# A round's second low-rank product moved up behind its first inverse, its tanh ahead of the group norm's root, and one weighted sum moved back

## The chip, the cores and the metric

The kernel runs on one core of a Trainium2 chip. The time is device microseconds of one execution, and several executions of each kernel are compared by their medians. The engines are TensorE (PE, products), VectorE (DVE), ScalarE (ACT), GpSimd (POOL) and SyncE (SP, which issues transfers). Each works through its own queue in order, and they wait for one another by semaphores.

## The reference

One layer, 512 tokens of 1024 features, 16 heads of 64. Cut to what the change touches:

```python
mod = (silu(c) @ w_ada + b_ada)                       # six vectors of 1024
p = (x * (1 + sc1) + sh1) @ w_in                      # pool, r, k, v, xw, xa, xg, two gates
w = -softplus(-(w0 + tanh(xw) @ w_decay_up)) - 0.5    # low-rank product, decay
a = sigmoid(a0 + xa @ w_aaa_up)                       # low-rank product, a
g = sigmoid(xg) @ w_gate_up
kk = heads(k * k_k); kk = kk / norm(kk)               # root and inverse
k = k * (1 + (a - 1) * k_a)
# per token: S = S*decay + (S @ -kk) (kk*a)^T + v k^T ;  o = S @ r
o = layer_norm(o, gn_g, gn_b, 64e-5)                  # group norm of a head, a root
o = o + sum(r * k * r_k) * v                          # the bonus
y_rwkv = (o * g) @ w_rwkv_up
# then the mix with the pool branch, layer norm, feed-forward (1024 x 4096), layer norm
```

## The kernel before

The heads are worked in four groups of four (QUADS = 4). A group is two halves q = 0 and 1 of 128 features each. The program for the recurrence runs rounds `it` from -1 to 4, each of 27 steps `s`, and each engine has a function `slot(it, s)` that says what it does in that step. The order is written by hand. In a round three groups are under way: `prep` prepares group it + 1 (low-rank products, decay, norms, keys), `work` solves group it in chunks of 64 tokens, and `tail` finishes group it - 1 (group norm, turn, gate). Round -1 only prepares, rounds 1 and 2 do all three, round 3 has no `prep`, round 4 only finishes. Round 0 has no `tail`.

Between these, TensorE runs pieces of the large product with w_in: a piece is 4 multiplies of 128x512 (line 1846), and PER_SLOT says how many pieces follow in each step: 3 in step 8, none in 9, 3 in 10, none in 11, 3 in 12. The weights of that product are split into a high part on ScalarE (line 790) and a low part on GpSimd (line 673); TensorE waits for the low part.

TensorE's results of the recurrence go to three accumulator sets in turn. The list PE_ORDER says in which order, and so which set an item takes (its place in the list modulo 3); an item waits until the one before it in the same set has been taken away.

The names that matter here, in the order of TensorE's steps:

- W0 (step 8), then inv0 (step 8, line 1965), the spread of the inverse norm of half 0, made by VectorE from a root on ScalarE; VectorE uses it in `unit_keys` (line 1313).
- bonus (step 9, line 1983); VectorE takes it at line 1424.
- D (step 10, line 1888).
- lora1 (lines 1947 and 1948), the low-rank products of half 1. ScalarE takes them in `lora_tanh` (lines 852 and 853, into sg and aa_odd), VectorE sums the decays from sg (lines 1294 and 1297).
- K (step 12, line 1900), HD0 and HD1 (step 12, line 1924). VectorE adds one to K, which gives KI (line 1265).
- yT (step 13, line 1900, reads O), the turn of y; ScalarE copies it at line 996.
- norm1 (step 13, line 1955), the root of it on ScalarE (line 860), the inverse on VectorE (lines 1301 and 1304), inv1 on TensorE (step 15, line 1965).

The group norm's root is on ScalarE in step 9 (line 968). Tanh and exponential share one table of functions there, the root is in another, so each change between them has an ACT_TABLE_LOAD.

Beside that, the vectors `mod` of the second half of w_ada are summed on VectorE, eight weighted sums a round (line 1491, the first 1489), in the steps of ADA_USED. Their weights are loaded by ScalarE's queue in the steps of ADA_LOADED (line 909). Odd-numbered tiles share one place and even-numbered ones another, and a load waits until the sum before it in that place is done: the fifth load counted from zero waits for the sum counted three.

The lines that set this:

```python
ADA_LOADED = (1, 5, 7, 9, 12, 12, 14, 15)
ADA_USED = (4, 8, 10, 11, 13, 14, 16, 26)
ADA_COUNT = (1, 2, 1, 3, 2, 4, 3, 5)
```

Of the kernel before, what the change touches and what calls it, by code (L numbers as in the profile page):

```python
# [14 lines left out]
def build(nc, x, c, w_ada, b_ada, w_in, mu_shift, pool_mix, pool_scale, w_pool_up, w0, w_decay_up, a0,  # L15
# [5 lines left out]
    S, D = x.shape[1], x.shape[2]  # L21
# [24 lines left out]
    with ctx:  # L46
# [125 lines left out]
        def flat(t):  # L172
            return t[:, :, :, :].rearrange("p g c t -> p g (c t)")
# [12 lines left out]
        def blocks(t):  # L186
            return Q[:, t * BPT:(t + 1) * BPT, :]

        def flat_blocks(t):
            return blocks(t).rearrange("p b v -> p (b v)")  # L190
# [29 lines left out]
        def over16(m):  # L220
# [2 lines left out]
        QUADS = PAIRS // 2  # L223
        SLOTS = 27
        PE_ORDER = ["TB", "TK", "O", "BR0", "BR1", "lora0", "mod", "AT0", "AT1", "TV", "AD0", "AD1", "A2T", "norm0", "A4", "A4T",
                    "D1", "KR0", "KR1", "A8T", "D2", "W0", "inv0", "bonus", "D", "lora1", "K", "HD0", "HD1", "yT", "norm1", "gate",
                    "inv1", "V1", "K2", "TT", "AP0", "AP1", "MR0", "MR1", "N", "OI", "S1", "S2", "S3", "S4", "S5", "S6"]
        BY_ACT = ["TB", "TK", "LT0", "LT1", "TV", "A2T", "A4T", "D1", "D2", "W0", "D", "K", "HD0", "HD1", "V1", "TT", "AP0", "N", "OI"]
        BY_DVE = ["BR0", "BR1", "AT0", "AT1", "AD0", "AD1", "A2I", "A4", "A4I", "KR0", "KR1", "A8T", "KI", "K2", "AP1", "MR0", "MR1",
# [138 lines left out]
                seen[raw_of[k]] = (k, at + 1)  # L368
        ADA_LOADED = (1, 5, 7, 9, 12, 12, 14, 15)
        ADA_MIDDLE = 4  # L370
        ADA_USED = (4, 8, 10, 11, 13, 14, 16, 26)
        def ada_tile(kt):

            return flat_blocks(c1) if kt in (2, 4, 6) else y[:, KT - 2:KT, :].rearrange("p g t -> p (g t)")
# [391 lines left out]
        def _(act):  # L766
            counts = {}

            def link(ins, name=None):
                key = name or "act_step"  # L770
                counts[key] = counts.get(key, 0) + 1
                ins.then_inc(sem(key), 1)
                act.wait_ge(sem(key), counts[key])
# [137 lines left out]
            def slot(it, s):  # L911
                n = it + 1
                work, prep, tail = 0 <= it < QUADS, n < QUADS, it >= 1
# [55 lines left out]
                if s == 8:  # L969
                    if work:  # L970
                        keep(b6, "D2", it)
                        keep(c6, "W0", it)
                        wait_made(act, "KR1", it)
                    if tail and it < QUADS:
                        act.wait_ge(sem("centred"), it)
                        link(act.activation(flat_blocks(At), flat(O), ACT.Square), "o_squared")
                if s == 10 and prep:
                    squares(it, 1)
                if s == 10 and it == QUADS:
                    act.wait_ge(sem("gate_spread"), 1)  # L980
                    link(act.activation(gate1[:, :], pset[set_of("gate")][:, :, :].rearrange("p g t -> p (g t)"), ACT.Copy, scale=0.5), "gate_row")
                if s == 12:
                    if prep:
                        lora_tanh(it, 1)
                    if work:
                        load_ada(it, ADA_MIDDLE)
                        keep(b1, "K", it)
                        keep_pair(b2, b7, "HD0", it)
                        keep_pair(b2, b7, "HD1", it)
# [790 lines left out]
        def _(pe):  # L1780
# [224 lines left out]
            def slot(it, s):  # L2005
                work, prep, tail = 0 <= it < QUADS, it + 1 < QUADS, it >= 1
# [45 lines left out]
                if s == 8:  # L2052
                    if work:
                        wait_kept(pe, "A4", it)
                        wait_kept(pe, "A4T", it)
                        to_heads("A8T", it, [(b1, b2)])
                        wait_kept(pe, "D1", it)
                        wait_kept(pe, "A4I", it)
                        to_heads("D2", it, [(std(b4), b7)])
                        wait_kept(pe, "KR0", it)  # L2060
                        wait_kept(pe, "KR1", it)
                        wait_kept(pe, "TV", it)
                        to_heads("W0", it, [(c6, c5)])
                    if prep:
                        inverse_norm(it, 0)
                if s == 9 and work:
                    bonus(it)
                if s == 10 and work:
                    wait_kept(pe, "A8T", it)
                    wait_kept(pe, "D2", it)  # L2070
                    to_pairs("D", it, [(std(b5), b6)])
                if s == 11 and prep:
                    lora(it, 1)
                if s == 12 and work:
                    pe.wait_ge(sem("lt_masked"), it + 1)
                    wait_kept(pe, "D", it)
# [278 lines left out]
```

## Time and profile before

| | us |
|---|---|
| median of 3 runs | 1065.74 |
| lowest, highest | 1058.37, 1066.62 |
| profiled execution, its own time | 1067.4 |
| span of the profiled execution | 1065.7 |
| TensorE busy | 976.8 |
| VectorE busy | 677.8 |
| ScalarE busy | 467.0 |
| GpSimd busy | 378.1 |

The rounds lie about so in the span: round -1 from 72 us, 0 from 120, 1 from 212, 2 from 304, 3 from 402, 4 from 497 to 525. Behind them come the gates and up products, the output product and the feed-forward part, which the change does not touch. A number in brackets at the end of a row of a timeline is how long the engine sat idle before it, and who released it.

### The profile page before, as it was taken

Reading aid. Unit: us, or ns where it says so; the run is one execution under the profiler, and the core shown is the slowest. Engines: PE = TensorE matmul, PEld = TensorE weight load, DVE = VectorE, ACT = ScalarE, POOL = GpSimd, SP = SyncE. Lnnn points to the kernel's source line nnn. Section 1 sums busy time; section 2 is a strip of 40 time slices with the busy share of each in tenths; the row PEclk is TensorE's granted clock in tenths of the full one; section 3 lists DMA queues with packets and bytes.
Section 4 is the critical chain, followed back from the end, with each engine's and each line's share of the span. In section 5 each row is a group of like instructions: output and inputs, shape, how many; then the busy total and the mean of one; then the engine's idle time right before and its main releaser. Section 6 shows DMA issues by size and latency. Waiting matters only on the chain.

```text
span 1065.7 us, 27456 instructions
## 1 busy us (share of the span) xinstructions
PE 976.8 (92%) x11539; PEld 811.6 (76%) x11539; DVE 677.8 (64%) x929; ACT 467.0 (44%) x571; POOL 378.1 (35%) x226
## 2 busy tenths in 40 slices
PE   1798898999999899899999999798999999999994
PEld 1676786787768577767688888688898898998983
DVE  5734666658847876683223155467787787787877
ACT  0335354337534632444533243284545445445451
POOL 6332501321231132123544445245153351451532
PEclk9698998999999999999999999988999999999997
DMA  9331323334332333333344337222251432423201
GB/s 365 108 98 45 95 86 89 99 82 117 98 84 85 95 108 82 92 116 81 120 119 108 86 120 231 77 60 79 81 157 36 121 112 65 138 77 85 76 1 79
DMA packets 122919, 108.04 MB, mean 101 GB/s; under 512 B 5395, under 2 KB 104641, under 8 KB 122817
## 3 DMA queue, kind: packets, MB, share of 16 engines
q1 hardware_dynamic: 113009, 83.46, 26.2%
q10 hardware_dynamic: 9808, 23.08, 7.0%
q8 instruction: 81, 1.33, 0.5%
q14 instruction: 21, 0.17, 0.1%
HBM read 100.23 MB, written 2.10 MB: 96 GB/s over the span
## 4 chain that ended last, share of the span: by engine, by line
PE 69%; DVE 17%; ACT 5%; issue 3%; DMA 2%; POOL 2%; SPq 1%; ACTq 0%; DVEq 0%; POOLq 0%
PE bank L1846 12%; PE set L2208 11%; PE bank L2294 7%; PE set L2147 6%; PE bank L2147 5%; PE set L1900 4%; PE set L2294 4%; PE set L2246 3%; PE set L1888 3%; PE set L1912 2%; PE bank L2208 2%; PE bank L1827 2%; DVE a_sum L1516 1%; PE set L1924 1%; DVE w_lo L1557 1%
## 5 line engine op out<-in xcount | busy, mean ns | idle before, releaser
L673 POOL TENSOR_TENSOR w_lo<-w_raw,w_hi 128x1024 fp32r<-128x1024 f32 (+2 forms) x75 | 170.8, 2278 | 393.0 <-ACT w_hi L790 384.6
L790 ACT ACTIVATE w_hi<-w_raw 128x1024 fp32r<-128x1024 f32 (+2 forms) x81 | 81.8, 1010 | 107.3 <-PE set L2147 35.2
L819 ACT ACTIVATE Q<-set 128x1024 f32<-128x1024 f32 x56 | 57.4, 1025 | 138.2 <-PE set L1900 69.3
L1846 PE MATMUL bank<-h_hi,w_hi 128*128 128x512 f32 x256 | 110.3, 431 | 3.4 <-POOL w_lo L673 2.8
L1603 DVE SCALAR_TENSOR_TENSOR res<-set,mod,res 128x256 f32<-128x256 f32 x192 | 92.9, 484 | 26.3 <-PE set L2208 17.5
L2208 PE MATMUL set<-a_hi,w_hi 128*128 128x256 f32 x384 | 109.2, 284 | 0.0
L2208 PE MATMUL set<-a_lo,w_hi 128*128 128x256 f32 x384 | 108.9, 284 | 0.0
L2208 PE MATMUL set<-a_hi,w_lo 128*128 128x256 f32 x384 | 108.9, 283 | 0.0
L1846 PE MATMUL bank<-h_lo,w_hi 128*128 128x512 f32 x256 | 105.1, 411 | 0.0
L1146 ACT ACTIVATE w_hi<-w_raw 128x1024 fp32r<-128x1024 f32 x70 | 74.3, 1062 | 69.8 <-PE set L2208 64.3
L1846 PE MATMUL bank<-h_hi,w_lo 128*128 128x512 f32 x256 | 104.2, 407 | 0.7 <-issue 0.7
L733 POOL TENSOR_TENSOR w_lo<-w_raw,w_hi 128x1024 fp32r<-128x1024 f32 x38 | 91.5, 2408 | 9.8 <-POOL w_lo L733 5.9
L2208 PEld LDWEIGHTS set<-a_hi,w_hi 128*128 128x128 f32 x384 | 74.0, 193 | 0.5
L2208 PEld LDWEIGHTS set<-a_lo,w_hi 128*128 128x128 f32 x384 | 73.9, 193 | 0.3
L2208 PEld LDWEIGHTS set<-a_hi,w_lo 128*128 128x128 f32 x384 | 73.9, 193 | 0.0
L1846 PEld LDWEIGHTS bank<-h_hi,w_hi 128*128 128x128 f32 x256 | 50.1, 196 | 20.4 <-issue 5.9
L740 POOL TENSOR_TENSOR w_raw<-w_raw 128x1024 f32<-128x1024 f32 x8 | 19.4, 2422 | 116.8 <-DVE w_lo L1557 116.8
L1846 PEld LDWEIGHTS bank<-h_hi,w_lo 128*128 128x128 f32 x256 | 49.9, 195 | 11.8 <-issue 0.7
L1846 PEld LDWEIGHTS bank<-h_lo,w_hi 128*128 128x128 f32 x256 | 50.4, 197 | 9.9 <-issue 0.7
L1557 DVE TENSOR_TENSOR w_lo<-w_raw,w_hi 128x1024 fp32r<-128x1024 f32 x38 | 46.6, 1225 | 11.9 <-ACT w_hi L1146 9.2
L2294 PE MATMUL set<-h_hi,w_hi 128*128 128x512 f32 x128 | 49.8, 389 | 0.0
L2294 PE MATMUL set<-h_lo,w_hi 128*128 128x512 f32 x128 | 49.8, 389 | 0.0
(358 smaller groups left out, 2290.3 us busy)
## 6 DMA issues: line engine op xcount, KB each, us to landing
w_raw<-in_w_ff_dram SPq DMA_DIRECT2D x64, 512.0 KB, 4.0
w_raw<-in_w_in_dram SPq DMA_DIRECT2D x46, 512.0 KB, 3.8
y<-in_w_ada_dram ACTq DMA_DIRECT2D x20, 512.0 KB, 3.9
ada<-in_w_ada_dram SPq DMA_DIRECT2D x16, 512.0 KB, 9.9
Q<-in_w_ada_dram ACTq DMA_DIRECT2D x12, 512.0 KB, 4.1
w_raw<-in_w_rwkv_up_dram SPq DMA_DIRECT2D x8, 512.0 KB, 3.7
w_raw<-in_w_out_dram SPq DMA_DIRECT2D x8, 512.0 KB, 4.5
xtok<-in_x_dram SPq DMA_DIRECT2D x4, 512.0 KB, 10.2
```

The lines of the kernel that those rows point to most:

```text
L673: link(pool.tensor_tensor(part_of(k, w_lo), raw_part(k), part_of(k, w_hi).bitcast(F32), ALU.subtract), "lo_ready")
L733: link(pool.tensor_tensor(w_lo[SLOT[m]][:, :, :], raw[:, :, :], w_hi[SLOT[m]][:, :, :].bitcast(F32), ALU.subtract), "lo_ready")
L790: link(act.activation(part_of(k, w_hi), raw_part(k), ACT.Copy), "hi_ready")
L819: link(act.activation(by_half(tile), psum_flat(set_of(name)), ACT.Copy), "act_kept")
L1146: link(act.activation(w_hi[SLOT[m]][:, :, :], raw[:, :, :], ACT.Copy), "hi_ready")
L1557: link(dve.tensor_tensor(w_lo[slot][:, :, :], raw[:, :, :], w_hi[slot][:, :, :].bitcast(F32), ALU.subtract), "lo_by_dve")
L1603: link(dve.scalar_tensor_tensor(out=res[:, f, tokens], in0=product, scalar=mod[:, 40 + f:41 + f], in1=res[:, f, tokens], op0=ALU.mult, op1 ...
L1846: mm = pe.matmul(o, w, hx, start=(m == 0), stop=(m == 3 * KT - 1))
L1900: mm = pe.matmul(ps[N * p:N * p + N, q, c * C:(c + 1) * C], by_pair(left, p, q, c), by_pair(right, p, q, c), start=(m == 0), stop=(m == le ...
L2147: mm = pe.matmul(o, w[slot_of(k)][:, kt, :], hx[:, kt, :], start=(kt == 0 and m == 0), stop=(kt == kts - 1 and m == 2))
L2208: mm = pe.matmul(to, wx[:, i, columns], a[:, form, i, :], start=OPENS[at] and b == 0 and i == 0 and m == 0, stop=i == 1 and m == 2, skip_g ...
L2294: mm = pe.matmul(bank[m][:, :], w[slot][:, kt, :], hx[:, kt, :], start=(kt == 0 and at == 0), stop=(kt == KT - 1 and at == 2))
```

## The change

Three edits, each in the hand-written order.

1. lora1 goes from step 11 to step 8 on TensorE, right behind inv0. With it its place in PE_ORDER changes, so that lora1 takes set 2, bonus set 0 and D set 1 (before: bonus 2, D 0, lora1 1). bonus then waits for W0's copy, D for the use of inv0, K for the tanh pair of lora1, HD0 for the use of bonus, HD1 for D's copy.
2. The tanh pair of lora1 goes from step 12 to the end of step 8 on ScalarE, ahead of the copy and the weight split of step 9, D's copy and the group norm's root.
3. The weighted sum counted three goes from step 11 to step 12 on VectorE, behind KI and the decay sums.

```diff
-                    "D1", "KR0", "KR1", "A8T", "D2", "W0", "inv0", "bonus", "D", "lora1", "K", "HD0", "HD1", "yT", "norm1", "gate",
+                    "D1", "KR0", "KR1", "A8T", "D2", "W0", "inv0", "lora1", "bonus", "D", "K", "HD0", "HD1", "yT", "norm1", "gate",
...
-        ADA_USED = (4, 8, 10, 11, 13, 14, 16, 26)
+        ADA_USED = (4, 8, 10, 12, 13, 14, 16, 26)
...
                     if tail and it < QUADS:
                         act.wait_ge(sem("centred"), it)
                         link(act.activation(flat_blocks(At), flat(O), ACT.Square), "o_squared")
+                    if prep:
+                        lora_tanh(it, 1)
...
                 if s == 12:
-                    if prep:
-                        lora_tanh(it, 1)
                     if work:
...
                     if prep:
                         inverse_norm(it, 0)
+                        lora(it, 1)
...
-                if s == 11 and prep:
-                    lora(it, 1)
```

TensorE in round 0, around the first inverse (L1965), with lora1 (L1947, L1948), K (L1900) and the first HD (L1924); the pieces and the bonus product between are left out:

```order
 L1900 MATMUL set<-Q 64x64 x96
 L1965 MATMUL set<-ident,inverse 64x128 x8
+L1947 MATMUL set<-xwa,lup 128x512
+L1948 MATMUL set<-xwa,lup 128x512
...
-L1947 MATMUL set<-xwa,lup 128x512
-L1948 MATMUL set<-xwa,lup 128x512
 L1900 MATMUL set<-Q 64x64 x32
 L1924 MATMUL set<-Q 64x128 x32
```

lora1 now stands directly behind inv0, and K follows the pieces of step 10 directly.

VectorE in round 0, from the last of the scaled writes (L1340) to the inverse of norm1 (L1301); L1265 is KI, L1491 the weighted sums:

```order
 L1340 TENSOR_TENSOR Q<-t 128x2x256
-L1491 SCALAR_TENSOR_TENSOR y<-y,derived 128x1024
-L1265 TENSOR_TENSOR Q<-set,Q 128x1024
-L1294 TENSOR_SCALAR sg<-sg 128x512
-L1297 SCALAR_TENSOR_TENSOR t<-scanm,sg 128x512
+L1265 TENSOR_TENSOR Q<-set,Q 128x1024
+L1294 TENSOR_SCALAR sg<-sg 128x512
+L1297 SCALAR_TENSOR_TENSOR t<-scanm,sg 128x512
+L1491 SCALAR_TENSOR_TENSOR y<-y,derived 128x1024
 L1491 SCALAR_TENSOR_TENSOR y<-Q,derived,y 128x1024
 L1301 TENSOR_SCALAR norms<-norms 128x8
```

One sum went from ahead of KI to behind the decay sums, and stands next to the sum that follows.

ScalarE in round 1, from the square of the group norm (L976) to the second root (L860); L909 are the loads of weights, L996 the copy of the turn:

```order
 L976 ACTIVATE Q<-O 128x1024
+L852 ACTIVATE sg<-set,derived 128x512
+L853 ACTIVATE aa_odd<-set,derived 128x512
 L796 ACTIVATE G<-bank,derived 128x512
...
-L852 ACT_TABLE_LOAD
-L852 ACTIVATE sg<-set,derived 128x512
-L853 ACTIVATE aa_odd<-set,derived 128x512
...
 L996 ACTIVATE y<-set,params 128x512 x2
-L860 ACT_TABLE_LOAD
 L860 ACTIVATE norms<-set 128x8
```

The tanh pair went ahead of the root of step 9, and two table loads are gone. Round 2 shows the same; in rounds -1 and 0 the pair moves and no load goes.

## Rows read from the trace of the kernel before

**Rows 1.** The page, busy time by engine: us, share of the span, instructions
```profile
PE 976.8 (92%) x11539; PEld 811.6 (76%) x11539; DVE 677.8 (64%) x929; ACT 467.0 (44%) x571; POOL 378.1 (35%) x226
```

**Rows 2.** Waits of TensorE, 72 to 525 us: total us, times, longest us
```profile
PE set L1900 <- DVE Q L1265: 3.9, 3, 2.2
...
PE set L1924 <- ACT aa_odd L853: 2.5, 2, 1.3
```

**Rows 3.** Timeline of TensorE, round 1: start us, us, what, [idle before]
```profile
259.82 0.69 PE L1947 MATMUL set<-xwa,lup 64*128 64x512 f32 x1
...
260.88 1.16 PE L1900 MATMUL set<-Q 64*64 64x64 f32 x64
...
264.18 1.10 PE L1924 MATMUL set<-Q 64*64 64x128 f32 x32 [1.26 <-ACT aa_odd L853]
...
269.10 1.16 PE L1900 MATMUL set<-Q,O 64*64 64x64 f32 x64 [0.82 <-DVE Q L1265]
...
275.29 1.09 PE L1965 MATMUL set<-ident,inverse 128*64 128x128 f32 x16
```

**Rows 4.** Timeline of VectorE, round 1
```profile
255.95 1.22 DVE L1424 TENSOR_TENSOR xvb<-set,xvb 128x1024 f32<-128x1024 f32 x1 [1.69 <-PE set L1983]
...
266.40 1.28 DVE L1491 SCALAR_TENSOR_TENSOR y<-y,derived 128x1024 f32<-128x1024 f32 x1
267.72 1.22 DVE L1265 TENSOR_TENSOR Q<-set,Q 128x1024 f32<-128x1024 f32 x1
...
270.70 1.28 DVE L1491 SCALAR_TENSOR_TENSOR y<-Q,derived,y 128x1024 f32<-128x1024 f32 x1
```

**Rows 5.** Timeline of ScalarE, round 1
```profile
261.43 1.28 ACT L852 ACT_TABLE_LOAD   x1
262.72 0.69 ACT L852 ACTIVATE sg<-set,derived 128x512 f32<-128x512 f32 x1
...
267.83 0.34 ACTq L909 DMA_DIRECT2D y<-in_w_ada_dram  x1
270.32 1.59 ACT L996 ACTIVATE y<-set,params 128x512 f32<-128x512 f32 x2 [2.51 <-PE set L1900]
```

**Rows 6.** Timeline of three engines, round 0, from the bonus product on
```profile
169.07 1.23 DVE L1424 TENSOR_TENSOR xvb<-set,xvb 128x1024 f32<-128x1024 f32 x1 [4.98 <-PE set L1983]
...
179.14 0.34 ACTq L909 DMA_DIRECT2D y<-in_w_ada_dram  x1
...
179.56 1.28 ACT L860 ACT_TABLE_LOAD   x1 [0.45 <-ACT Q L825]
...
180.82 1.28 DVE L1491 SCALAR_TENSOR_TENSOR y<-Q,derived,y 128x1024 f32<-128x1024 f32 x1
...
182.60 1.09 PE L1965 MATMUL set<-ident,inverse 128*64 128x128 f32 x16 [1.96 <-DVE inverse L1304]
...
184.40 1.30 DVE L1491 SCALAR_TENSOR_TENSOR y<-y,derived 128x1024 f32<-128x1024 f32 x1 [1.86 <-DMA y<-in_w_ada_dram]
```

**Rows 7.** Timeline of TensorE, round -1, and one operation of GpSimd in it
```profile
88.53 0.79 PE L1846 MATMUL bank<-h_hi,w_hi 128*128 128x512 f32 x1 [1.99 <-POOL w_lo L673]
...
92.02 0.39 PE L1846 MATMUL bank<-h_hi,w_lo 128*128 128x512 f32 x1
...
95.78 0.69 PE L1947 MATMUL set<-xwa,lup 64*128 64x512 f32 x1
...
90.55 2.67 POOL L673 TENSOR_TENSOR w_lo<-w_raw,w_hi 128x1024 fp32r<-128x1024 f32 x1 [2.07 <-ACT w_hi L790]
```

**Rows 8.** Timelines of VectorE and TensorE, round 3, before the turn
```profile
454.59 1.28 DVE L1491 SCALAR_TENSOR_TENSOR G<-y,derived,G 128x1024 f32<-128x1024 f32 x1
...
458.40 1.36 PE L1900 MATMUL set<-Q,O 64*64 64x64 f32 x64 [2.23 <-DVE Q L1265]
```

**Rows 9.** Stretches: us, busy us (instructions) of each engine, TensorE's granted clock, DMA share, GB/s
```profile
88.50:90.00 1.50, 1.47 (x4) 1.18 (x5) 1.23 (x3) 1.44 (x3) 0.00 (x0) 0.50 0.15 32
...
458.40:459.50 1.10, 1.10 (x61) 1.00 (x64) 1.03 (x3) 0.00 (x0) 0.00 (x0) 1.00 0.77 242
```

## The prediction

> **What bounds the kernel now.** I read the share of busy time first, then the waits of TensorE over the stretch with the rounds, then the timelines of single rounds. The span is TensorE's: it is busy 92% of it [rows 1]. What the change can win is therefore idle time of TensorE in the rounds -1 to 4, between 72 and 525 us, and two lines of its waits there bear on the moved code [rows 2]: 3.9 us for VectorE's Q, and 2.5 us for the tanh in aa_odd, the wait that the moved product is about. The timelines decide whether it goes or only turns into another.
>
> Round 1 shows how these waits hang together (round 2 repeats it within 0.1 us). TensorE idles 1.26 us before the second half of HD, and 0.82 us before the turn of y [rows 3]. The first idle waits for aa_odd, which ScalarE makes late because it has just taken a root and must load a table first [rows 5]. The second waits for KI on VectorE, the operation at 267.72 [rows 4]. VectorE itself started that run of work at 255.95, after waiting 1.69 us for the bonus product of TensorE, and works from there almost without a gap to the end of KI [rows 4]. So between the bonus product and the turn, VectorE is what TensorE ends up waiting for, and VectorE's run starts with the bonus product.
>
> **The change, part by part.** The second low-rank product takes 1.06 us of TensorE (259.82 to the next product at 260.88) [rows 3]. It isn't removed: it moves ahead of twelve weight multiplies and the bonus product. So the bonus product comes 1.06 us later, and VectorE's run with it. The weighted sum that moves behind KI takes 1.32 us with its gap (266.40 to 267.72) [rows 4], and leaves the run ahead of KI by as much.
>
> *Rounds 1 and 2.* KI moves 1.06 us later and 1.32 us earlier: 0.26 us earlier. TensorE arrives at the turn 1.26 us sooner, since the tanh is now long done, and waits there 0.82 + 1.26 - 0.26 = 1.82 us in one piece. The gain is 0.26 us in each round, not 2. The two tables that go in each of these rounds (the one before the tanh is at 261.43 [rows 5]) are ScalarE's time, and ScalarE has a new wait in their place. Its fifth transfer of weights, issued at 267.83 [rows 5], overwrites the tile that the moved sum reads. It now stands until that sum is done, which is when the next sum can begin: 270.70 before [rows 4], and 1.06 later by the bonus product, 271.76. Behind it in ScalarE's queue are the turn's copy (270.32) and the second root. The copy starts at 272.1, 1.8 us later; the table load of 1.28 us behind it is gone; so the root is 0.5 us later. Between the turn's start at 269.10 and the second inverse product at 275.29 TensorE has its own products without a gap [rows 3], of which the inverse needs the first two only; a root 0.5 us later is covered by them. Two rounds: -0.5 us.
>
> *Round 0.* Here there is no group norm, so no table is saved. VectorE waited 4.98 us for the bonus product, started at 169.07 and was held by nothing until its sum at 180.82 was done, at 182.10; TensorE idled 1.96 us for the inverse that followed, and began the second inverse product at 182.60, 0.5 us behind VectorE's sum [rows 6]. With the bonus product 1.06 us later the sum starts at 181.88, the moved one having just ended. Only then may ScalarE issue the fifth transfer, before at 179.14; behind it stands the table load for the root, before at 179.56. Transfer, load and root take 0.34 + 1.28 + 0.2, to 183.7 [rows 6], and 0.5 us later, at 184.2, TensorE resumes: +1.6. The same transfer was used 5.26 us after its issue (179.14 to 184.40); now it lands at 187.1, and VectorE loses 2.7 us there. Bounds: +1.06 (only the bonus product counts) and +2.7 (the late transfer counts whole). TensorE is itself 1.6 later and has weight multiplies behind the inverse product, so I take +1.6, the sum of the rows in between.
>
> *Round -1.* After the first inverse product TensorE idles 1.99 us for a low half on GpSimd (88.53) [rows 7]. The moved product fits into it: -1.06. Some 0.95 us of idle are left, no more than the 0.82 and 1.26 us that changed no clock in round 1. Before, the clock fell: the granted clock is 0.50 behind 88.5 us, 1.2 of 2.4 GHz [rows 9]. Eight multiplies from 88.53 to 92.02 took 3.49 us, the sixteen from there to 95.78 took 0.235 each, so the low clock cost 3.49 - 1.88 = 1.6 us [rows 7]. Against that, the tanh pair (0.69 us each [rows 5]) now stands ahead of the high half from which the next low half is made; that one began at 90.55, took 2.67 us [rows 7], and now ends at 94.6, where TensorE would want it at 88.53 + 24 x 0.235 = 94.2. Sum: -1.06 - 1.6 + 0.4 = -2.2 us. If the clock falls all the same it is -1.06, and with no clash at the low half -2.7. I take -2.2, since the idle that stays is nearest to those that cost nothing.
>
> *Round 3.* No product is moved (no round follows that needs it). Only the sum of 454.59 goes behind KI. TensorE idled 2.23 us before the turn, for KI [rows 8]; what was last there comes 1.28 us sooner, so -1.3 us. Bounds: -1.3, and 0 should another wait stand right behind it. I take -1.3, as the 2.23 us are longer than what leaves.
>
> The accumulator sets that change hands have no price of their own: the bonus product now waits for W0 to be copied, D for the first inverse to be used, K for the tanh pair. Between W0 and the bonus product stand two small products and twelve multiplies, some 5 us by the steps above; the other two are older still. Gone, that cover would cost at most what one such wait did, 1.26 us a round. On SyncE's queue the reload of the low-rank weights waits for the moved product, which now comes sooner.
>
> Sum: -2.2 + 1.6 - 0.5 - 1.3 = -2.4 us. Against the profiled execution's own 1067.4 that is 1065.0. That execution lies 1.7 us above the median of the runs, 1065.74; for the median it gives **1063.3 us**. What a measurement can tell from no change is about 1%, 1055.1 to 1076.4.
>
> **Rivals.** *The single idle drops the clock (slower).* In rounds 1 and 2 two idles of 1.26 and 0.82 us become one of 1.8 us before the turn. Behind 1.99 us in round -1 the clock went to 0.50 and cost 1.6 us [rows 7, 9]. Twice that is +3.2, which gives 1066.5, and 1067.6 where round -1 keeps its low clock too. It decides where the multiplies behind the turn run at 1.2 GHz. Against it: in round 3, before the same turn, 2.23 us of idle left the clock at 1.00 [rows 8, 9]. The Trainium skill (TensorE: Matmul & The Clock Gate, What's actually happening) has the clock follow how busy the engine was of late, not one wait alone; that 1.99 us fell and 2.23 us did not agrees. Chance 0.2.
>
> *VectorE has slack.* If its run could start without the bonus product, rounds 1 and 2 would win all their idle, 2 x 2.08 us, and round 0 would lose nothing: -2.2 - 4.2 - 1.3 = -7.7, 1058.0. VectorE's waits of 1.69 and 4.98 us for exactly that product speak against it [rows 4, 6]. Chance 0.1.
>
> *The tables count.* Four loads go. If ScalarE set the pace there, each would return 1.28 us: -5.1, 1060.6. Against it: TensorE's waits for aa_odd are 2.5 us in all [rows 2], and what the tables give is taken by the wait for the reload. Chance 0.05. The Trainium skill (ScalarE: Activation LUTs, What ACT_TABLE_LOAD costs) puts a switch at 2.66 us, its drain counted; by that this rival would give 1055.1. In this trace the tanh starts 1.29 us after its load does [rows 5], and shows no drain.
>
> *Nothing to be seen.* The order is as the change says, but stalls that come and go (the runs lie between 1058.37 and 1066.62) cover it: 1065.7. Chance 0.1. The forecast has the remaining 0.55.
>
> **The numbers.** The cases lie between 1058.0 and 1067.6; with the spread of the runs at the upper end I take 1057.5 to 1068.0 for 8 in 10. Faster by over 1% needs -10.7 us, which VectorE's slack reaches only with a lucky median: 0.05. Slower by over 1% needs +10.7 us, more than the clock falling in every round: 0.03. Within 1%: 0.92.
>
> **What would show it.** Right: in rounds 1 and 2 no idle before HD and one of about 1.8 us before the turn, released by VectorE; ScalarE's copy of the turn directly behind the fifth transfer; in round 0 about 3.5 us of idle before the second inverse product instead of 1.96; in round 3 0.9 us before the turn instead of 2.23; round -1 at full clock behind 88.5 us. Wrong: if the idle before the turn vanishes, VectorE was not what binds; if round 0's second inverse product is not later, ScalarE's wait for the reload costs nothing; if the clock is at 0.5 behind the turn in rounds 1 and 2, the first rival holds.

## The result and the profile after

| | before | after |
|---|---|---|
| median of 20 executions each, us | 1065.29 (1057.74 to 1072.29) | 1073.86 (1066.27 to 1080.13) |
| ratio, with its 95% interval | 1 | 1.0081 (1.006 to 1.0102) |
| profiled execution and its span, us | 1067.4, 1065.7 | 1072.69, 1071.0 |
| mean granted clock of TensorE, profiled execution | 0.964 | 0.962 |
| the same, mean over executions | 0.972 (94, run beside the experiments) | 0.963 (20) |

The change makes the kernel 0.8% slower, by 8.6 us of median. That is less than the 1% that I had set as the bound of no change, but it is outside my range of 1057.5 to 1068.0, and on the wrong side: I had forecast 2.4 us less. (The comparison leaves out executions that lie far above the fastest of their kernel, three of the eleven in e4 below.) The profiled execution of before has a lower clock than its executions mostly have, and the two profiles differ by 5.3 us only.

The page of the kernel after looks like that of before [rows 1]: the same instructions in TensorE, four fewer in ScalarE (the tables), and hardly more busy time.

```profile
PE 979.6 (91%) x11539; PEld 811.0 (76%) x11539; DVE 678.5 (63%) x929; ACT 462.2 (43%) x567; POOL 383.0 (36%) x226
```

The wait of TensorE for KI over the rounds, 72 to 535 us (total us, times, longest), answers to [rows 2]:

```profile
PE set L1900 <- DVE Q L1265: 5.0, 3, 2.1
```

The wait for the tanh is gone, as intended; that for VectorE's KI has grown from 3.9 to 5.0 us and sits in the turn of y. The rounds 1 and 2 on TensorE (start us, us, what, [idle before]) answer to [rows 3]:

```profile
266.67 1.16 PE L1900 MATMUL set<-Q,O 64*64 64x64 f32 x64 [2.05 <-DVE Q L1265]
...
273.89 2.19 PE L1888 MATMUL set<-Q 64*64 64x64 f32 x128
...
364.99 1.96 PE L1900 MATMUL set<-Q,O 64*64 64x64 f32 x64 [2.06 <-DVE Q L1265]
...
378.50 3.69 PE L1888 MATMUL set<-Q 64*64 64x64 f32 x128
382.12 0.50 PE L1846 MATMUL bank<-h_hi,w_hi 128*128 128x512 f32 x1
```

These are the rows to look at. Both rounds have the same idle in the same place, 2.05 and 2.06 us. In round 1 the turn and what follows it take about what they took before: 7.22 us from the turn to the next group of 64x64 products, as before, and 2.19 us for that group (2.09 before). In round 2 every duration in that stretch is nearly twice as long: 13.51 us to the group, and 3.69 us for it. The stretches show why (us, busy us and instructions of PE, PEld, DVE, ACT and POOL, granted clock, DMA share, GB/s):

```profile
268.00:272.00 4.00, 4.00 (x15) 1.73 (x15) 2.88 (x4) 1.86 (x4) 0.00 (x0) 1.00 0.32 91
...
364.99:382.12 17.13, 17.13 (x224) 10.55 (x224) 8.96 (x10) 6.46 (x10) 2.75 (x1) 0.50 0.36 102
...
382.00:384.00 2.00, 2.00 (x16) 1.58 (x10) 1.64 (x2) 0.69 (x1) 0.00 (x0) 0.96 0.71 172
```

The granted clock is 0.50 (1.2 of 2.4 GHz) from the turn at 364.99 to the first weight multiply at 382.12: 17.13 us. I call such a change from 1.00 to 0.50 a fall of the clock. TensorE is busy all that time: the same products take 9.34 us in round 1, from the turn at 266.67 to the weight multiply at 276.01. The next two views show the rest of round 1 on VectorE and on ScalarE (its queue's own rows are ACTq), which answer to [rows 4, 5]:

```profile
254.85 1.22 DVE L1424 TENSOR_TENSOR xvb<-set,xvb 128x1024 f32<-128x1024 f32 x1 [2.78 <-PE set L1983]
...
265.30 1.22 DVE L1265 TENSOR_TENSOR Q<-set,Q 128x1024 f32<-128x1024 f32 x1
```

```profile
269.65 0.34 ACTq L909 DMA_DIRECT2D y<-in_w_ada_dram  x1
270.04 1.59 ACT L996 ACTIVATE y<-set,params 128x512 f32<-128x512 f32 x2 [3.34 <-DVE y L1491]
271.66 0.18 ACT L860 ACTIVATE norms<-set 128x8 f32<-128x8 f32 x1
```

VectorE waits 2.78 us for the bonus product instead of 1.69, that is 1.09 longer (forecast 1.06), and KI starts 10.45 us behind the start of its run instead of 11.77. ScalarE's copy of the turn comes directly behind the fifth transfer, 3.37 us behind the turn's start instead of 1.22, and the root follows without a table. In round 0 the same transfer holds the root, its table load included (ScalarE, TensorE and VectorE, to [rows 6]):

```profile
176.14 0.33 ACTq L909 DMA_DIRECT2D y<-in_w_ada_dram  x1
...
176.56 1.28 ACT L860 ACT_TABLE_LOAD   x1 [3.37 <-DVE y L1491]
...
178.59 1.98 PE L1965 MATMUL set<-ident,inverse 128*64 128x128 f32 x16 [3.71 <-DVE inverse L1304]
...
179.84 2.86 DVE L1491 SCALAR_TENSOR_TENSOR y<-y,derived 128x1024 f32<-128x1024 f32 x1 [1.30 <-DMA y<-in_w_ada_dram]
```

TensorE's idle there is 3.71 us instead of 1.96, and it too goes with a low clock (the second inverse product takes 1.98 us instead of 1.09; the clock is at 0.50 from 177.2 to 184.2, where the kernel before had it low only behind that place, for about half as long). Round -1 went as forecast: the low half is waited for 0.94 us instead of 1.99, and the clock stays (to [rows 7, 9]).

```profile
87.89 0.50 PE L1846 MATMUL bank<-h_hi,w_hi 128*128 128x512 f32 x1 [0.94 <-POOL w_lo L673]
...
100.14 1.09 PE L1965 MATMUL set<-ident,inverse 128*64 128x128 f32 x16 [2.11 <-DVE inverse L1304]
```

```profile
88.00:90.00 2.00, 2.00 (x9) 1.66 (x10) 1.85 (x4) 1.94 (x3) 0.00 (x0) 1.00 0.40 99
...
178.60:182.00 3.40, 3.40 (x72) 3.07 (x76) 2.16 (x1) 3.06 (x4) 2.36 (x1) 0.50 0.11 46
```

In round 3 the idle before the turn is what I said (to [rows 8]):

```profile
463.59 1.25 PE L1900 MATMUL set<-Q,O 64*64 64x64 f32 x64 [0.91 <-DVE Q L1265]
```

Where the time went in the profiled execution is read off the bonus product, which starts once a round. Before it stood at 167.07, 253.96, 351.06 and 444.41; now:

```profile
162.34 1.88 PE L1983 MATMUL set<-G,ones_head 128*128 128x512 f32 x4
...
252.86 1.88 PE L1983 MATMUL set<-G,ones_head 128*128 128x512 f32 x4
...
351.17 1.88 PE L1983 MATMUL set<-G,ones_head 128*128 128x512 f32 x4
...
450.94 1.88 PE L1983 MATMUL set<-G,ones_head 128*128 128x512 f32 x4
```

The kernel after is 4.7 us ahead in round 0, 1.1 ahead in round 1, 0.1 behind in round 2 and 6.5 behind in round 3. Of the 4.7 us, 2.0 are the first idle of round -1, which the forecast has, and 0.6 were there ahead of it. The other 2.1 come behind it and are luck of these two executions for the most part: the idle before the second inverse product of round -1 is 2.11 us in both, but only before did the clock fall there (1.98 us for the product, and 0.50 behind it; after, 1.09 us at 100.14). Before:

```profile
102.76 1.98 PE L1965 MATMUL set<-ident,inverse 128*64 128x128 f32 x16 [2.11 <-DVE inverse L1304]
```

The 3.6 us lost from round 0 to round 1 hold the longer wait for the root and the clock behind it. The 6.4 us lost from round 2 to round 3 hold the clock's fall in round 2.

### The profile page after: what moved, and what is told of

Same layout as the page of the kernel before. It is cut to its first block, busy times and chain, and to the rows that moved or that the text cites. A ratio compares the mean times of both kernels' runs of the same rounds, so it can differ in the third digit from the quotient of the medians.

```text
span 1071.0 us, 27451 instructions
## 1 busy us (share of the span) xinstructions
PE 979.6 (91%) x11539; PEld 811.0 (76%) x11539; DVE 678.5 (63%) x929; ACT 462.2 (43%) x567; POOL 383.0 (36%) x226
## 4 chain that ended last, share of the span: by engine, by line
PE 66%; DVE 19%; ACT 6%; issue 4%; POOL 2%; DMA 2%; SPq 1%; ACTq 0%; DVEq 0%; POOLq 0%
PE bank L1846 11%; PE set L2207 11%; PE bank L2293 7%; PE set L2146 6%; PE bank L2146 5%; PE set L2293 4%; PE set L1900 3%; PE set L2245 3%; PE set L1888 2%; PE bank L2207 2%; PE set L1912 2%; PE bank L1827 2%; DVE a_sum L1516 1%; DVE Q L1265 1%; PE set L1924 1%
## 5 line engine op out<-in xcount | busy, mean ns | idle before, releaser
L1846 PE MATMUL bank<-h_hi,w_hi 128*128 128x512 f32 x256 | 108.1, 422 | 5.3 <-POOL w_lo L673 2.8
L2207 PE MATMUL set<-a_lo,w_hi 128*128 128x256 f32 x384 | 108.6, 283 | 0.0
L2207 PE MATMUL set<-a_hi,w_lo 128*128 128x256 f32 x384 | 108.6, 283 | 0.0
```

Source lines behind the costliest of these rows:

```text
L1846: mm = pe.matmul(o, w, hx, start=(m == 0), stop=(m == 3 * KT - 1))
L2207: mm = pe.matmul(to, wx[:, i, columns], a[:, form, i, :], start=OPENS[at] and b == 0 and i == 0 and m == 0, stop=i == 1 and m == 2, skip_g ...
```

## The experiments

Two theories stood against each other, with two rivals. **The clock:** two short idles that were harmless became one of 2 us, and behind it TensorE falls to half its clock for the whole stretch of products up to the next weight multiplies. **The reload:** ScalarE, held by the fifth transfer, delays the root and the copies behind it. **The tables** and **VectorE's slack** are the rivals of the prediction. A ratio is against the kernel before on the same chip; its median there was 1067.2 for e1 to e4, 1064.85 for e5 to e8, and 1064.98 for e9 to e12. Line numbers in rows are those of the experiment's own kernel and shift by a few where lines were added.

### e1: the sum alone

```diff
 (on the kernel before)
-        ADA_USED = (4, 8, 10, 11, 13, 14, 16, 26)
+        ADA_USED = (4, 8, 10, 12, 13, 14, 16, 26)
```

> The kernel before with the weighted sum moved behind KI (step 11 to 12) and nothing else. Theory A (the loss of the change is TensorE's clock, which falls behind the one long idle before the turn of y in rounds 1 and 2): here the idle before HD stays (1.26 us) and the one before the turn shrinks from 0.82 to 0, so no idle is longer than before; rounds 1, 2 gain 0.8 us each, round 3 gains 1.3, round 0 loses about 0.5 for ScalarE's wait for the reload: -2.5 us against before, -11 against the change. Theory B (ScalarE's wait for the reload of the weights, which this sum now releases late, is what costs): the wait is all here, so +5 to +8 us against before.

Measured: 1066.14, ratio 0.9978 (0.9947 to 1.001). TensorE in round 0 and in round 1, and the stretch behind the turn of round 1:

```profile
176.97 1.98 PE L1965 MATMUL set<-ident,inverse 128*64 128x128 f32 x16 [3.29 <-DVE inverse L1304]
...
265.12 1.16 PE L1900 MATMUL set<-Q,O 64*64 64x64 f32 x64
```

```profile
267.00:271.00 4.00, 4.00 (x11) 1.28 (x10) 1.91 (x2) 2.84 (x4) 0.00 (x0) 1.00 0.41 131
```

The sum alone takes the idle before the turn away, and the reload's wait in round 0 is there without the product: 3.29 us, 1.3 more than before. The reload theory asked for +5 to +8 us here; the ratio leaves no room for that. It isn't this part that makes the change slow.

### e2: the product alone

```diff
 (on the kernel after)
-        ADA_USED = (4, 8, 10, 12, 13, 14, 16, 26)
+        ADA_USED = (4, 8, 10, 11, 13, 14, 16, 26)
```

> The change without the moved sum: product and tanh pair moved, the sum back in step 11. Theory A: the single idle before the turn grows by 1.3 us to about 3.4 us in rounds 1 and 2, and the clock falls behind it each time: 2 x (7.7 + 1.3) and 1.3 in round 3 that are not gained, against -2 in round -1: +12 to +18 us against before, slower than the change. Theory B (the wait for the reload costs): that wait is gone, so the time is that of before or up to 3 us less.

Measured: 1085.59 (1083.01 to 1088.14), ratio 1.0162 (1.0115 to 1.0209), the slowest of all. The second inverse product of round 0, the turns of rounds 1, 2 and 3, and stretches behind two of them:

```profile
176.50 1.98 PE L1965 MATMUL set<-ident,inverse 128*64 128x128 f32 x16 [5.00 <-DVE inverse L1304]
...
266.30 1.99 PE L1900 MATMUL set<-Q,O 64*64 64x64 f32 x64 [3.38 <-DVE Q L1265]
...
372.37 1.99 PE L1900 MATMUL set<-Q,O 64*64 64x64 f32 x64 [3.38 <-DVE Q L1265]
...
470.46 1.99 PE L1900 MATMUL set<-Q,O 64*64 64x64 f32 x64 [2.53 <-DVE Q L1265]
```

```profile
268.30:276.00 7.70, 7.70 (x15) 3.19 (x15) 2.49 (x4) 5.33 (x7) 2.75 (x1) 0.50 0.11 25
...
282.30:282.90 0.60, 0.60 (x48) 0.55 (x40) 0.00 (x0) 0.60 (x1) 0.00 (x0) 1.00 1.12 339
...
472.00:480.00 8.00, 8.00 (x27) 2.26 (x19) 2.63 (x4) 2.61 (x3) 2.34 (x1) 0.50 0.22 66
```

Three turns, three falls of the clock. This kernel has no wait for the reload, so the slowness needs none. It also has the four tables saved, and nothing of that is seen in its time (e9 tests the tables without the falls). Nor has VectorE slack: the idle before the turn grew to 1.26 + 0.82 + 1.06 = 3.1 us and a little more (3.38). In round 0 the product alone lengthens the idle too: 5.00 us, of which 2.0 are a step of VectorE (line 1301) that here took 2.20 us instead of 0.17, and the other 1.0 are the product's.

### e3: the idle of the turn filled with weight multiplies

The multiplies of the weights are handed out by step; one group more goes to step 12, ahead of the turn, and is taken from step 15.

```diff
 (on the kernel after)
         def pieces_in(it, s):
+            if it in (1, 2) and s in (12, 15):
+                return {12: 5, 15: 1}[s]
             return (LAST_SLOTS if it == QUADS else PER_SLOT)[s]
```

> The change with two pieces of the large product (8 multiplies of 128x512, about 1.9 us) moved from step 15 to step 12 in rounds 1 and 2, so that TensorE has work where it idled before the turn. Theory A: the idle there shrinks from 2.05 to about 0.2 us, the clock holds, and each of the two rounds gives back the 1.9 us and, where it fell, about 7.7 us: -12 to -15 us against the change, 1059 to 1062. Theory B (the reload): ScalarE's wait and what hangs on it are as in the change, so only the 1.9 us a round come back, -4 us.

Measured: 1065.47 (1063.92 to 1070.19), ratio 0.9982 (0.9955 to 1.001). TensorE in rounds 1 and 2, and two stretches:

```profile
275.83 1.65 PE L1902 MATMUL set<-Q 64*64 64x64 f32 x64 [1.86 <-DVE Q L1267]
...
366.34 1.41 PE L1902 MATMUL set<-Q,O 64*64 64x64 f32 x64 [0.24 <-DVE Q L1267]
```

```profile
276.50:279.50 3.00, 3.00 (x43) 2.49 (x37) 2.86 (x5) 1.02 (x1) 1.86 (x1) 0.50 0.65 235
...
368.00:374.00 6.00, 6.00 (x43) 2.80 (x46) 4.81 (x6) 4.17 (x6) 1.27 (x1) 1.00 0.31 89
```

With the idle gone the clock stays at 1.00 behind both turns (over 265 to 272 too), and the loss is gone. The miss is in the size: the filled idle itself should have come on top. It came back further on instead: TensorE now waits 1.86 us at 275.83 for VectorE's next product operand, where the group that was taken away had stood, and the clock is at 0.50 behind that idle, over 276.5 to 279.5. Since e3 also changes the order of useful work, it does not isolate the clock. e9 does.

### e4: the same idle made in the kernel before

```diff
 (on the kernel before)
+            if it in (1, 2) and s in (12, 15):
+                return {12: 2, 15: 4}[s]
```

> The kernel before with one piece (4 multiplies, 0.94 us) moved away from step 12 to step 15 in rounds 1 and 2: TensorE comes to the turn 0.94 us sooner and idles 1.8 us there, in addition to the 1.26 us before HD. Product, tanh and sum are where they were. Theory A: the clock falls behind the turn in most executions, +1.9 without any fall and about +7.7 for each fall: +6 to +17 against before. Theory B: no wait of ScalarE is touched, only the 0.94 us a round are lost: +2.

Measured: median 1075.13 (1062.38 to 1081.78), ratio 1.0031 (0.999 to 1.0072). By the ratio it can't be told apart from before, so the forecast of +6 to +17 us is not confirmed by it; the median of all eleven executions lies 7.9 us above that of before. Turns of rounds 1, 2 and 3, and stretches behind the first two:

```profile
265.66 1.16 PE L1902 MATMUL set<-Q,O 64*64 64x64 f32 x64 [1.77 <-DVE Q L1267]
...
366.32 1.16 PE L1902 MATMUL set<-Q,O 64*64 64x64 f32 x64 [1.74 <-DVE Q L1267]
...
465.05 1.16 PE L1902 MATMUL set<-Q,O 64*64 64x64 f32 x64 [2.52 <-DVE Q L1267]
```

```profile
267.60:272.00 4.40, 4.40 (x12) 1.37 (x14) 2.56 (x4) 4.29 (x6) 0.81 (x1) 1.00 0.01 4
...
370.00:376.00 6.00, 6.00 (x7) 1.50 (x6) 1.60 (x3) 4.21 (x6) 2.75 (x1) 0.50 0.09 19
```

The product is where it was, and a longer idle before the turn is enough for the low clock. It also shows what I had not reckoned with: 1.74 us of idle fell in round 2, 1.77 us did not in round 1, and 2.52 us did not in round 3. An idle of this size is a chance of a fall, not a fall. In round 2 the turn itself (1.16 us at 366.32) still ran at full clock, and only the products behind it were slow. The Trainium skill (TensorE: Matmul & The Clock Gate, What's actually happening) says that the clock follows how active the engine was of late; that the idle alone doesn't decide agrees. But the same products stand ahead of both turns, so this sentence doesn't tell either which of them falls.

### e5: the fill, and the reload out of ScalarE's way

```diff
 (on e3)
-        ADA_USED = (4, 8, 10, 12, 13, 14, 16, 26)
+        ADA_USED = (4, 8, 10, 12, 13, 15, 16, 26)
+                if s == 14 and work:
+                    load_ada(it, ADA_MIDDLE + 1)
...
-                if work and s == 12:
-                    load_ada(it, ADA_MIDDLE + 1)
```

> The third experiment (the change with two pieces filled in before the turn of rounds 1 and 2) and, in addition, ScalarE's fifth transfer of weights issued behind the second root (step 14) instead of ahead of it (end of step 12), with its sum one step later on VectorE. Theory A (what is left of the change's loss is ScalarE's wait for the reload in round 0): the idle before round 0's second inverse product shrinks from 3.7 to about 2.4 us, the clock may still fall there; -1 to -1.5 us against the third experiment. Rival: VectorE's run sets that idle by itself and it stays at 3 us or more: no difference.

Measured: 1070.6 (1067.16 to 1075.46), ratio 1.0055 (1.0027 to 1.0083): a miss. TensorE, rounds 0 and 1:

```profile
178.71 1.42 PE L1967 MATMUL set<-ident,inverse 128*64 128x128 f32 x16 [3.00 <-DVE inverse L1306]
...
281.35 0.47 PE L1848 MATMUL bank<-h_hi,w_hi 128*128 128x512 f32 x1 [2.27 <-DVE xvb L1232]
```

The idle before the inverse product fell from 3.73 (in e3) to 3.00 us only, and a later transfer in the same queue now waits ahead of the copy that frees the bank of the weight multiplies: 2.27 us of new idle in each of the rounds 1 and 2. The wait was moved, not removed.

### e6, e7, e8: the bonus product first

The product stands directly behind the bonus product, so that VectorE's run isn't delayed; e7 adds the fill, e8 the edit of e5.

```diff
 (e6, on the kernel before)
-  ... "inv0", "bonus", "D", "lora1", "K", ...
+  ... "inv0", "bonus", "lora1", "D", "K", ...
-        ADA_USED = (4, 8, 10, 11, 13, 14, 16, 26)
+        ADA_USED = (4, 8, 10, 12, 13, 14, 16, 26)
+                if s == 9 and prep:
+                    lora_tanh(it, 1)          # ScalarE, was in step 12
+                if s == 9 and prep:
+                    lora(it, 1)               # TensorE, was in step 11
 (e7, on e6)
+            if it in (1, 2, 3) and s in (12, 15):
+                return {12: 4, 15: 2}[s]
```

> The low-rank product moved up less far: behind the bonus product (step 9), its tanh ahead of D's copy, the sum moved as in the change. Theory A (the bonus product starts VectorE's run, so it must not be delayed): the idle before HD is gone and the one before the turn is about 0.8 us in rounds 1 and 2, where the change has 2.05, so the clock holds; 1.3 us a round and 1.3 in round 3 won, 0.5 to 1.3 lost in round 0: -3 us against before, -11 against the change. Rival (it is the product's leaving step 11 that costs, by whatever way): as slow as the change.

> The sixth experiment with one piece of the large product (0.94 us) moved from step 15 to step 12 in rounds 1, 2 and 3, into what is left of the idle before the turn. Theory A: 0.6 to 0.8 us less in each of the three rounds, -2 us against the sixth. Rival (other waits stand right behind): no difference.

> The seventh experiment with the fifth transfer issued behind the second root as in the fifth experiment. Theory A: 1 us less in round 0, about -1 us against the seventh, and -5 to -6 us against before: about 0.5% faster than it.

Measured: e6 1064.71, ratio 0.999 (0.9965 to 1.0015); e7 1061.76 (1055.39 to 1066.24), ratio 0.9971 (0.9947 to 0.9995); e8 1064.33, ratio 1.0 (0.9979 to 1.0021). The turn of round 2 in e6 with the first gate products, and two stretches:

```profile
360.37 1.16 PE L1900 MATMUL set<-Q,O 64*64 64x64 f32 x64 [1.01 <-DVE Q L1265]
...
362.38 2.01 PE L2001 MATMUL set<-xg,lup 128*128 128x512 f32 x2
```

```profile
360.40:362.50 2.10, 2.10 (x73) 2.03 (x74) 2.03 (x3) 0.00 (x1) 0.00 (x0) 0.99 0.03 8
362.50:365.00 2.50, 2.50 (x4) 0.81 (x4) 2.05 (x2) 1.23 (x2) 0.00 (x0) 0.50 0.29 52
```

The single idle is 1.01 us instead of 2.05: the 1.06 us of the product, which here no longer stand ahead of VectorE's run. It isn't harmless either. In round 2 the clock fell 2.0 us behind the turn's start, with TensorE busy in between; in round 1, with the same idle of 1.01 us, it did not. So the length of the idle alone doesn't say whether the clock falls. That the small products of the turn have a share in it would fit the place of the fall, but is not shown. By the ratios (0.999 against 1.0081) e6 is some 9.7 us faster than the kernel after, with the product and its tanh one step later than there. e8 has the new wait of e5 again (0.81, 1.75 and 1.76 us) and by the medians loses what e7 won; the intervals overlap.

### e9: throw-away multiplies in the idle

This one settles the cause. Four multiplies whose results nobody reads are put into the idle before the turn, in rounds 1 and 2. No useful work moves.

```diff
 (on the kernel after)
+                        if it in (1, 2):
+                            wait_set_free(pe, "norm1", it)
+                            for _ in range(4):
+                                pe.matmul(pset[set_of("norm1")][:, 0, :], h_hi[:, 0, 0:P], h_hi[:, 0, :], start=True, stop=True)
```

> The change with four extra multiplies of 128x512 (about 0.95 us, their result is thrown away) on TensorE in the idle before the turn of rounds 1 and 2, in the accumulator set that norm1 takes next, once HD0 has been copied from it. No useful work is moved and nothing is released sooner: the idle of 2.05 us only becomes one of about 1 us and a stretch of multiplies. Theory A (the loss is the clock that falls behind the long idle): the clock holds behind the turn, and 5 to 9 us of the change's loss come back: 1063 to 1068. Rival (the third experiment gained by the work it moved, and the loss is in the order itself): 1072 to 1075, as the change.

Measured: 1064.66 (1060.22 to 1072.28), ratio 1.0003 (0.9973 to 1.0033), against 1.0081 for the same kernel without them: 0.78% or 8.3 us back. TensorE in round 2, and the stretch behind its turn (round 1 has the same 1.07 us of idle):

```profile
361.07 1.20 PE L2088 MATMUL set<-h_hi 128*128 128x512 f32 x4 [1.07 <-ACT Q L825]
362.20 1.16 PE L1900 MATMUL set<-Q,O 64*64 64x64 f32 x64
...
371.45 0.50 PE L1846 MATMUL bank<-h_hi,w_hi 128*128 128x512 f32 x1
```

```profile
364.20:368.40 4.20, 4.20 (x10) 1.17 (x10) 3.05 (x5) 2.87 (x5) 0.00 (x0) 1.00 0.40 125
```

The idle of about 2.1 us has become 1.07 us of idle and 1.1 us of throw-away work; the turn comes 13.96 us behind the bonus product instead of 13.82, 0.14 us later. From the turn to the first weight multiply round 2 takes 371.45 - 362.20 = 9.25 us, where the kernel after took 17.13. That is the price of this fall: **7.9 us**. Read the same way, the falls of e2 in rounds 1 and 2, of e4 and of e6 cost 6.1 to 7.4 us. The change of e9 also has the tables saved: the rival of the tables would put it at 0.9952 of before, outside its interval.

### e10, e11, e12: the best order, and what of it is order

```diff
 (e10, on e7)
+            table = {-1: {14: 2, 15: 1}, 0: {14: 2, 15: 1}, 1: {12: 4, 15: 2}, 2: {12: 4, 15: 2}, 3: {12: 4, 15: 2}}
+            if it in table and s in table[it]:
+                return table[it][s]
+                used = (4, 8, 10, 11, 13, 14, 16, 26) if it == 0 else ADA_USED
 (e11: the same table on the kernel before.
  e12: on the kernel after, with {12: 5, 15: 1} in rounds 1 and 2)
```

> The seventh experiment (product behind the bonus product, sum behind KI, one piece moved to step 12 in rounds 1 to 3) with the sum left in step 11 in round 0, where it holds the reload, and two pieces moved from step 15 to step 14 in rounds -1 and 0, between norm1 and the second inverse product, where TensorE idles about 2 us. Theory A: those idles go and the clock falls no more behind them: 1.3 + 1.9 + 1.9 us and up to 1.6 for each fall, -5 to -8 us against the seventh, about 0.9% faster than before. Rival (the pieces delay the norm or the inverse's turn by as much): no difference to the seventh.

> The kernel before with only the pieces moved as in the tenth experiment; product, tanh and sum where they were. Theory A: the two idles of about 2 us in rounds -1 and 0 are filled (-3.8 us and up to 3.2 of clock), and of the 0.82 us before the turn in rounds 1 and 2 and 2.23 in round 3 another -2.6: -6 to -9 us against before. If it is as fast as the tenth, the changed order adds nothing to filled idles; I expect the tenth 2 us faster.

> The change with all its idles filled by pieces (two in step 14 in rounds -1 and 0, two in step 12 in rounds 1 and 2, one in round 3). Theory A: without long idles the change loses to the tenth only what the later bonus product and the reload cost in round 0: 1 to 3 us slower than the tenth, 4 us or more faster than before. Rival (the order of the change is bad in itself): no faster than before.

Measured: e10 1060.36 (1057.37 to 1062.91), ratio 0.9948 (0.9918 to 0.9978); e11 1063.17 (1059.3 to 1066.7), ratio 0.9981 (0.995 to 1.0011); e12 1065.22 (1061.2 to 1074.73), ratio 1.0 (0.9969 to 1.0032). TensorE in e10, round -1:

```profile
105.42 0.47 PE L1850 MATMUL bank<-h_hi,w_hi 128*128 128x512 f32 x1 [2.63 <-DVE xvb L1233]
```

e10 is faster than both kernels, by 0.5% against before. The fills alone (e11) are not told apart from before; the medians put the order at 2.8 us on top of them, but the intervals of e10 and e11 overlap. e10 won less over e7 than expected, since the fill of round -1 turned into a wait of 2.63 us for the bank, and e12 has that same wait. e12 is 4.9 us of median above e10, where 1 to 3 us were expected. The two differ in the place of the product, in the sum of round 0 and in one piece, and their intervals just overlap, so what of it is the late bonus product is not shown.

## Why the prediction was wrong

**What held.** By its own steps: no idle before HD and one before the turn, released by VectorE, 2.05 and 2.06 us where I said 1.82. The bonus product delays VectorE's run by 1.09 us (1.06). The copy of the turn stands behind the fifth transfer, and the root needs no table. Round 0's idle is 3.71 us (3.5); the sum alone lengthens it by 1.3 us (e1), the product alone by 1.0 (e2), and together they make 1.75, since their waits overlap. Round 3's idle is 0.91 us (0.9), and from its bonus product to its turn 12.65 us pass instead of 13.99: -1.3, as said. In round -1 the way from the first inverse product to the first norm product went from 14.27 to 12.28 us: -2.0 (-2.2), at full clock. e9, the change with the falls taken out, has a ratio of 1.0003 (0.9973 to 1.0033); my forecast of -2.4 us would be 0.9977, inside that interval, but so is no change at all.

**What failed** is the rival *the single idle drops the clock*, in its chance and in its price: the sum that gave -2.4 us has no term for the clock behind the turn, and the rival that has one was given 0.2 and 1.6 us a fall. The sign I had named for it, a clock of 0.5 behind the turn, showed in round 2.

Its chance, 0.2, rested on one row: round 3's 2.23 us of idle at a clock of 1.00 [rows 8, 9]. One execution of one round doesn't show that an idle is harmless. In e4 two idles that differ by 0.03 us, before the same instruction in the same execution, ended differently, and in the kernel after round 2 fell and round 1 did not. In the trace of before, the clock had fallen behind 1.99 us [rows 7, 9] and behind 2.11 us (102.76). With harmless and harmful examples of nearly the same idle, even odds for each of the two rounds would have been the sober reading.

Its price, 1.6 us a fall, was taken from round -1, where the low clock lasted for eight weight multiplies, 3.49 us. Behind the turn stand the turn itself, the norm product, eight gate multiplies of 512 columns, the inverse product and 128 small ones. All of them ran at half the clock: 17.13 us instead of 9.25 (e9). That is 7.9 us for this fall, five times my price. Had I followed the timeline of round 1 from the turn at 269.10 [rows 3] on to the next weight multiplies and doubled that stretch, instead of carrying a price from another place, the rival would have read -2.4 + 7.9 = +5.5 us for one fall and +13.4 for both. The median of +8.6 lies between the two. It would also have shown that slower by over 1% needs no more than two falls; I had written that it needs more than the clock falling in every round. In the profiled execution one round fell, and it is 5.3 us above that of before.

The clock is missing from my sum in round 0 as well. I forecast an idle of 3.5 us there and gave it no price beyond the wait. From the bonus product of round 0 to that of round 1 the kernel before took 86.89 us and the kernel after 90.52: +3.6, where my terms give +1.6. The low clock lasts 6.8 us in that stretch instead of 3.4; half of the difference, 1.7 us as an estimate, is most of the rest.

Rounds 1 and 2 of all fourteen read so (one execution each; a fall is where the first two gate products take 1.85 to 2.06 us instead of 1.10):

| idle right before the turn | kernels | rounds | falls |
|---|---|---|---|
| none, up to 0.26 us | e1, e3, e5, e7, e8, e10, e11, e12 | 16 | 0 |
| 0.82 and 0.87 us | before | 2 | 0 |
| 1.07 us and four throw-away multiplies | e9 | 2 | 0 |
| 1.01 us | e6 | 2 | 1 |
| 1.74 to 2.06 us | after, e4 | 4 | 2 |
| 3.38 us | e2 | 2 | 2 |

As far as so few rounds tell, the longer the idle, the likelier the fall. My bound for round -1, "no more than the 0.82 and 1.26 us that changed no clock in round 1", was the same mistake on a smaller scale: behind 1.01 us the clock fell once in two.

The profiles show one execution of each kernel, but the mean granted clock is on record for every execution. With a mean clock c, a share of 2 x (1 - c) of the span was at 1.2 GHz, and where TensorE was busy, half of that time is lost. As an estimate (idle counted as if it were work):

| kernel | executions | mean clock | lost to the clock, us | mean time less that, us |
|---|---|---|---|---|
| before | 94 | 0.972 | 29.8 | 1035.9 |
| after | 20 | 0.963 | 39.4 | 1034.7 |
| e9 | 12 | 0.975 | 26.8 | 1037.6 |
| e2 | 6 | 0.954 | 49.5 | 1036.2 |
| e4 | 11 | 0.964 | 38.5 | 1035.7 |

The change loses 9.6 us more to the clock than before, somewhat more than one fall of 17 us in each execution would cost, and gains 1.2 us in the rest, on the side of my forecast of 2.4 but not told apart from nothing. e2 and e4 are slow in the last column no more than the others: their price is the clock too.

**The other rivals.** VectorE's slack is refuted: the idle moved to the turn and grew in e2. The tables are refuted by e9, which has them gone and no fall behind the turn in its profile, and yet is not faster than before. That the change does nothing is refuted by the interval.

**Open.** TensorE also stands still for some us in places where the profile names no releaser (issue): 3.09 us ahead of 156.47 in the kernel after, 2.32 ahead of 309.59. The clock fell behind these too. Why they come, and in which executions, was not tested. The executions of before spread over 14.6 us, those of after over 13.9. By the same estimate the slowest quarter of the 94 executions of before lost 36.6 us to the clock and the fastest 24.2, while their times differ by 9.9 us; so the spread goes with the clock. Where in the kernel it falls, and so in how many executions rounds 1 and 2 do, the mean does not say. Which idles of 1 to 2.5 us bring a fall stays open.

## What to carry to other kernels

Before joining two short idles of TensorE into one, look at what stands behind the join: if the clock can fall there, the price is the stretch of products behind it (13.6 to 17.1 us at half the clock behind this turn), read at that place and not carried from another. One harmless example in one execution isn't proof; four multiplies thrown away in the idle test the question at 0.14 us a turn. And a product put ahead of the one that starts another engine's run delays that run by its own length: here it was better directly behind it (e6, e7, e10).

## What the runs showed of the hardware

- The same idle before the same turn can end both ways in one execution: 1.01 and 1.01 us (e6), 1.77 and 1.74 us (e4), 2.05 and 2.06 us (after). In round 3, 2.52 us kept the clock (e4) and 2.53 us lost it (e2).
- The clock can fall behind the idle and not in it: 2.0 us later, in a stretch of TensorE without a gap (e6, 362.38).
- A fall can last long though TensorE is busy without a gap: 17.13 us at 0.50 behind 364.99, in products of the turn, the gate and the inverse; the clock was back with the first weight multiply at 382.12 (0.96 over 382 to 384). It isn't the weight multiplies alone that bring it back: in e2 it was at 1.00 over 282.3 to 282.9, ahead of the first of them at 282.92, and in round -1 of before it stayed at 0.50 through those behind 104.67 until about 108.6:

```profile
106.00:108.00 2.00, 2.00 (x6) 1.52 (x6) 1.21 (x3) 0.60 (x1) 0.00 (x0) 0.50 0.40 102
```

- A table load took 1.28 us in this trace (176.56), and the four that the change saved are not seen in the time of e9.
